# Feed-forward's second product in four chunks, by seven block products instead of eight, three of them kept in PSUM

## What is computed

```python
def rms_norm(x, g):
    xf = x.astype(jnp.float32)
    y = xf * lax.rsqrt(jnp.mean(xf * xf, axis=-1, keepdims=True) + EPS)
    return (y * g.astype(jnp.float32)).astype(x.dtype)
...
    x = x + rms_norm(merged @ w_o, norm_mix_post)
    hf = rms_norm(x, norm_ff_pre)
    ff = jnp.square(jax.nn.relu(hf @ w_ff_in)) @ w_ff_out
    return x + rms_norm(ff, norm_ff_post)
```

## Time and profile before

| what | us |
|---|---|
| median of 3 runs | 802.95 |
| the three runs | 802.93, 804.87, 802.95 |
| the profiled execution, its own time | 805.02 |
| the span of the trace in it | 803.3 |
| PE busy in the span | 790.7 (98%) |
| DVE busy | 415.5 (52%) |
| ACT busy | 322.2 (40%) |

### The profile page before, as it was taken

The page is one execution under the profiler, slowest core; times in us unless marked ns, Lnnn a source line. Parts: engine busy times, 40 slices in busy tenths (PEclk is TensorE's granted clock), DMA queues, the critical chain, the costliest instruction groups (busy, mean ns, idle before and its releaser), DMA issues.

```text
span 803.3 us, 10375 instructions
## 1 busy us (share of the span) xinstructions
PE 790.7 (98%) x3736; PEld 660.4 (82%) x3736; DVE 415.5 (52%) x730; ACT 322.2 (40%) x561; POOL 60.4 (8%) x110
## 2 busy tenths in 40 slices
PE   7999999999999999999999999999999999999996
PEld 6888888888887888888888988888888888888885
DVE  5624667777777238866536654442323354432334
ACT  4522656656565742232344444322112344322211
POOL 2000000122232003000002300000000000000001
PEclk8999999999999999999999999999999999999999
DMA  8243222212222631345231343322323333322202
GB/s 288 87 124 104 77 82 78 80 53 85 74 79 59 204 99 59 105 149 184 87 104 47 87 134 126 104 100 84 105 82 103 94 89 104 104 82 103 78 1 104
DMA packets 96214, 80.22 MB, mean 100 GB/s; under 512 B 3120, under 2 KB 77872, under 8 KB 96176
## 3 DMA queue, kind: packets, MB, share of 16 engines
q1 hardware_dynamic: 95504, 79.70, 31.6%
q10 hardware_dynamic: 672, 0.01, 0.0%
HBM read 77.60 MB, written 2.10 MB: 99 GB/s over the span
## 4 chain that ended last, share of the span: by engine, by line
PE 96%; DVE 2%; DMA 1%; ACT 1%; issue 0%; SPq 0%; DVEq 0%; POOLq 0%; POOL 0%; ACTq 0%
PE acc L1126 30%; PE acc L1127 30%; PE acc L1128 30%; PE aux L1313 1%; DMA g_pre<-in_norm_mix_pre 1%; PE aux L1239 1%; PE aux L1238 1%; PE aux L1248 1%; PE acc L1267 1%; PE acc L1264 1%; PE aux L1221 1%; PE aux L1168 1%; DVE x L819 0%; DVE actB_lo L810 0%; ACT probs L673 0%; DVE scores_sb L939 0%
## 5 line engine op out<-in xcount | busy, mean ns | idle before, releaser
L800 DVE TENSOR_TENSOR w_lo<-w_raw,w_hi 128x1024 fp32r<-128x1024 f32 x132 | 161.4, 1224 | 199.9 <-ACT w_hi L564 199.3
L564 ACT ACTIVATE w_hi<-w_raw 128x1024 fp32r<-128x1024 f32 x132 | 138.9, 1054 | 192.4 <-PE acc L1128 190.2
L1126 PE MATMUL acc<-actB_hi,w_hi 128*128 128x512 f32 (+1 forms) x544 | 207.0, 381 | 0.0
L1128 PE MATMUL acc<-actB_hi,w_lo 128*128 128x512 f32 (+1 forms) x544 | 205.2, 377 | 0.0
L1127 PE MATMUL acc<-actB_lo,w_hi 128*128 128x512 f32 (+1 forms) x544 | 205.0, 377 | 0.0
L1128 PEld LDWEIGHTS acc<-actB_hi,w_lo 128*128 128x128 f32 x544 | 102.4, 188 | 19.1
L1127 PEld LDWEIGHTS acc<-actB_lo,w_hi 128*128 128x128 f32 x544 | 102.5, 188 | 18.2
L1126 PEld LDWEIGHTS acc<-actB_hi,w_hi 128*128 128x128 f32 x544 | 102.4, 188 | 18.1
L1126 PE MATMUL acc<-w_hi,ff_hi 128*128 128x512 f32 x256 | 101.0, 395 | 0.0
L1128 PE MATMUL acc<-w_hi,ff_lo 128*128 128x512 f32 x256 | 101.0, 395 | 0.0
L1127 PE MATMUL acc<-w_lo,ff_hi 128*128 128x512 f32 x256 | 101.0, 394 | 0.0
(11 more groups left out here) (163 smaller groups left out, 895.9 us busy)
## 6 DMA issues: line engine op xcount, KB each, us to landing
w_raw<-in_w_in SPq DMA_DIRECT2D x44, 512.0 KB, 3.8
w_raw<-in_w_ff_in SPq DMA_DIRECT2D x32, 512.0 KB, 4.0
w_raw<-in_w_ff_out SPq DMA_DIRECT2D x32, 512.0 KB, 3.7
w_raw<-in_w_b SPq DMA_DIRECT2D x8, 512.0 KB, 3.5
w_raw<-in_w_a SPq DMA_DIRECT2D x8, 512.0 KB, 3.5
w_raw<-in_w_o SPq DMA_DIRECT2D x8, 512.0 KB, 3.7
x<-in_x SPq DMA_DIRECT2D x4, 512.0 KB, 7.5
x<-in_x SPq DMA_DIRECT2D x1, 2048.0 KB, 8.3
```

The source lines that it names most:

```text
L564: nc.scalar.activation(w_hi[:, j], w_raw[:, j], ACT.Copy).then_inc(hi_made, 1)
L800: nc.vector.tensor_tensor(w_lo[:, j], w_raw[:, j], w_hi[:, j].bitcast(F32), ALU.subtract).then_inc(lo_made, 1)
L1126: nc.tensor.matmul(o, a_hi, b_hi, start=first, stop=False)
L1128: return nc.tensor.matmul(o, a_lo, b_hi, start=False, stop=last)
```

## The change

**The products.** The second product is cut into 2 x 2 blocks: the tokens in two halves (0 to 255, 256 to 511), the inner dimension into even and odd tiles of 128, the output columns in two halves. With A for the activations and B for `w_ff_out`, the seven products are

- P1 = A11 B11, P2 = A12 B21, P4 = A22 T4, P3 = S4 B22
- P5 = S1 T1, P6 = S2 T2, P7 = S3 T3
- S1 = A21 + A22, S2 = S1 - A11, S3 = A11 - A21, S4 = A12 - S2
- T1 = B12 - B11, T2 = B22 - T1, T3 = B22 - B12, T4 = T2 - B21

and every output block is a sum of some of them. The S and T are made by DVE. The sums S, 256 wide per pair of tiles, lie in `s_raw`; their rounded and rest parts go to `op_hi` (in the region where `actA` and then `ff_sum` lay) and `op_lo` (in the region of `ff_hi` and `ff_lo`). T1, T2 and T4 lie in `t_raw`, which is slots 2 and 3 of `w_raw`; T3 overwrites B12 in `down_raw`.

**The chunks.** The 32 tiles go in four chunks of eight. A chunk is eight units of `w_ff_in` as before, and then the seven products in the order of `PRODUCTS`, each as two items (h = 0, 1) of 12 matmuls. Units and items share the ring of four slots of `w_hi` and `w_lo`; the numbers n = 0 to 21 are the 22 entries of a chunk. `w_ff_in` is now loaded into slots 0 and 1 of `w_raw` alone, and `w_ff_out` for a chunk as four transfers of 1 MB into `down_raw`.

**PSUM.** P5, P7 and P3 keep their two banks each over all four chunks. P1, P6, P4 and P2 share banks 0 and 1 of `acc` with each other and, from the second chunk on, with the `w_ff_in` units. Each of the four is taken out once a chunk (semaphore `taken`): by ACT copies in the first, by DVE additions in the second and third, by the merges in the last.

The diff, cut to its core:

```diff
@@ -76,9 +76,33 @@
...
-HALF_K = FF // P // 2
-U_HALF = 2 * HALF_K
-UNITS = U_FF + 2 * U_HALF
...
+CHUNKS = 4
+FF_UNITS = FF // P // CHUNKS
+PAIRS = FF_UNITS // 2
+PRODUCTS = ["P1", "P5", "P6", "P7", "P4", "P3", "P2"]
+ITEMS = FF_UNITS + 2 * len(PRODUCTS)
+UNITS = U_FF + CHUNKS * ITEMS
+LEFT = {"P1": 0, "P2": 1, "P4": 2, "P5": 3, "P6": 4, "P7": 5, "P3": 6}
+ROTATING = ["P1", "P6", "P4", "P2"]
+SUMS = ["T1a", "T1b", "T3a", "T2a", "T2b", "T3b", "T4a", "T4b"]
...
-            for c in range(2):
-                first = U_FF + c * U_HALF
-                with sp.Fori(0, HALF_K // SLOTS) as i:
-                    for j in range(SLOTS):
-                        slot_free(i * SLOTS + (first + j))
-                        load_columns(j, w_ff_in_v, bass.ds(i * (SLOTS * P) + (c * HALF_K + j) * P, P))
...
-                    for n in range(HALF_K // 2):
-                        slot_free(h * (HALF_K // 2) + (first + HALF_K + n))
-                        load_rows(n % SLOTS, w_ff_out_v, c * HALF_K + 2 * n, bass.ds(h * COL, COL))
...
+            def load_up(m):
+                if m < SLOTS:
+                    slot_free(U_FF + m)
+                else:
+                    before = m - 4 if m < 6 else m - 2
+                    sp.wait_ge(lo_made, U_FF + ff_unit(before) + 1)
+                load_columns(m if m < SLOTS else m % 2, w_ff_in_v, slice(m * P, (m + 1) * P))
+
+            def load_down(c, j):
+
+                if c:
+                    sp.wait_ge(lo_made, U_FF + item(c, 0))
+                elif j >= 2:
+                    sp.wait_ge(turned, T_FF + TT)
+                k = c * FF_UNITS + 2 * j
+                sp.dma_start(down_raw[:, j], w_ff_out_v[:, k:k + 2, :]).then_inc(down_loaded[j], 16)
...
+            for c in range(1, CHUNKS):
+                for n in range(FF_UNITS):
+                    load_up(c * FF_UNITS + n)
+                    if 2 <= n < 2 + PAIRS:
+                        load_down(c, n - 2)
...
+            for c in range(CHUNKS):
+                for n in range(FF_UNITS):
+                    m, j = c * FF_UNITS + n, n // 2
+                    act.wait_ge(pe_done, UNIT_DONE[U_FF + item(c, n)])
+                    if m >= 4:
+                        act.wait_ge(op_lo_made, 3 * ((m - 4) // 2 + 1))
+                    bank = n % (4 if c == 0 else 2)
+                    nc.scalar.activation(ff_act[:, m % 4], acc[:, bank], ACT.Relu).then_inc(relu_made, 1)
+                    hi_ahead(item(c, n))
+                    act.wait_ge(sq_made, m + 1)
+                    if n % 2 == 0:
+                        nc.scalar.activation(op_hi[:, j, 0], ff_act[:, m % 4, 0:2 * P],
+                                             ACT.Copy).then_inc(op_hi_made, 1)
+                    else:
+                        nc.scalar.activation(op_hi[:, j, 1:3].rearrange("p a s -> p (a s)"), ff_act[:, m % 4],
+                                             ACT.Copy).then_inc(op_hi_made, 1)
+                        act.wait_ge(s_made, 4 * (c * PAIRS + j + 1))
+                        nc.scalar.activation(op_hi[:, j, 3:7].rearrange("p a s -> p (a s)"),
+                                             s_raw[:].rearrange("p a s -> p (a s)"),
...
-                                                 ).then_inc(ssq_act, 1)
-                        if h == 0:
-                            for j in range(SLOTS):
-                                hi_of(UNITS - SLOTS + j)
+                        hi_ahead(product_item(c, name, h))
...
+                o, x, y = {"T1": (t, b12, b11), "T3": (b12, b22, b12), "T2": (t, b22, t), "T4": (t, t, b21)}[name[:2]]
...
+                for n in range(FF_UNITS):
+                    m, j = c * FF_UNITS + n, n // 2
+                    f = ff_act[:, m % 4]
+                    dve.wait_ge(relu_made, m + 1)
+                    nc.vector.tensor_tensor(f, f, f, ALU.mult).then_inc(sq_made, 1)
+                    lo_ahead(item(c, n))
+                    dve.wait_ge(sq_made, m + 1)
+                    if n % 2 == 0:
+                        if m >= 2:
+                            dve.wait_ge(op_hi_made, 3 * (c * PAIRS + j))
+                        nc.vector.tensor_tensor(s_raw[:, 2], f[:, 0:2 * P], f[:, 2 * P:S],
+                                                ALU.subtract).then_inc(s_made, 1)
+                        if n == 2:
+                            weight_sum(c, "T1a")
+                        if n == 4:
+                            weight_sum(c, "T1b")
+                        if n == 6:
+                            weight_sum(c, "T3a")
+                        if n == 0 and last:
+                            dve.wait_ge(taken, 8 * c)
+                            merge(sum2[:], sum2[:], sum1[:])
+                            merge(sum6[:], sum6[:], sum1[:])
+                        dve.wait_ge(op_hi_made, 3 * (c * PAIRS + j) + 1)
+                        nc.vector.tensor_tensor(op_lo[:, j, 0], f[:, 0:2 * P], op_hi[:, j, 0].bitcast(F32),
+                                                ALU.subtract).then_inc(op_lo_made, 1)
+                        if n == 6:
...
+                        e = ff_act[:, (m - 1) % 4]
+                        count = 4 * (c * PAIRS + j)
+                        nc.vector.tensor_tensor(s_raw[:, 0], e[:, 2 * P:S], f[:, 2 * P:S],
+                                                ALU.add).then_inc(s_made, 1)
+                        dve.wait_ge(s_made, count + 2)
+                        nc.vector.tensor_tensor(s_raw[:, 1], s_raw[:, 0], e[:, 0:2 * P],
+                                                ALU.subtract).then_inc(s_made, 1)
+                        dve.wait_ge(s_made, count + 3)
+                        nc.vector.tensor_tensor(s_raw[:, 3], f[:, 0:2 * P], s_raw[:, 1],
+                                                ALU.subtract).then_inc(s_made, 1)
+                        dve.wait_ge(op_hi_made, 3 * (c * PAIRS + j) + 2)
+                        nc.vector.tensor_tensor(op_lo[:, j, 1:3].rearrange("p a s -> p (a s)"), f,
+                                                op_hi[:, j, 1:3].rearrange("p a s -> p (a s)").bitcast(F32),
+                                                ALU.subtract).then_inc(op_lo_made, 1)
+                        dve.wait_ge(op_hi_made, 3 * (c * PAIRS + j) + 3)
+                        dve.wait_ge(s_made, count + 4)
+                        nc.vector.tensor_tensor(op_lo[:, j, 3:7].rearrange("p a s -> p (a s)"),
+                                                s_raw[:].rearrange("p a s -> p (a s)"),
+                                                op_hi[:, j, 3:7].rearrange("p a s -> p (a s)").bitcast(F32),
+                                                ALU.subtract).then_inc(op_lo_made, 1)
...
+                for name in PRODUCTS:
+                    for h in range(2):
+                        at = FF_UNITS + 2 * PRODUCTS.index(name) + h
+                        for made in {8: ["T2b"], 9: ["T3b"], 10: ["T4a"], 11: ["T4b"]}.get(at, []):
+                            weight_sum(c, made)
+                        lo_ahead(item(c, at))
+                    if 0 < c and not last and name in ROTATING:
+                        dst = {"P1": sum1, "P6": sum6, "P4": sum4, "P2": sum2}[name]
+                        for p in range(2):
+                            bank_done(name, p)
+                            nc.vector.tensor_tensor(dst[:, p], acc[:, p], dst[:, p], ALU.add).then_inc(taken, 1)
...
+                    if name == "P1":
+                        merged_so_far()
+                        for p in range(2):
+                            bank_done(name, p)
+                            merge(sum2[:, p], acc[:, p], sum2[:, p])
+                            merge(sum6[:, p], acc[:, p], sum6[:, p], signal=taken)
...
+                    if name == "P3":
+                        for p in range(2):
+                            bank_done(name, p)
+                            merge(sum1[:, p], aux[:, 2 + p], sum1[:, p], signal=ff_ready)
+                        for p in range(2):
+                            gain(4 + p, sum1[:, p], 1, p)
+                        for t in (2, 3):
+                            dve.wait_ge(rstd_ff, t - 1)
+                            dve.wait_ge(gained, 4)
+                            nc.vector.scalar_tensor_tensor(x1[:, t], down_raw[:, t, 0], rstd[:, 4, t:t + 1], x1[:, t],
+                                                           ALU.mult, ALU.add).then_inc(y_made, 1)
...
+            for p in range(2):
+                dve.wait_ge(pe_done, BANK_DONE[UNITS - 1, p])
+                nc.vector.tensor_tensor(sum2[:, p], acc[:, p], sum2[:, p], ALU.add).then_inc(ff_ready, 1)
+                gain(6 + p, sum2[:, p], 0, p)
+                dve.wait_ge(rstd_ff, 3 + p)
...
+            BANKS = {"P1": acc[:, 0:2], "P6": acc[:, 0:2], "P4": acc[:, 0:2], "P2": acc[:, 0:2],
+                     "P5": acc[:, 2:4], "P7": aux[:, 0:2], "P3": aux[:, 2:4]}
+
+            def bank_free(c, name, p):
+
+                if name in ROTATING:
```

(33 more changed lines are left out.)

349 lines of the change are left out of this document (215 added, 134 removed).

## The result

The changed kernel takes 811.03 us (median of four runs, 810.79 to 811.57). The kernel before takes 802.98 us beside it: ratio 1.0095, 95% interval 1.0078 to 1.0113. The forecast was 806.4 us in a range of 796.0 to 813.0. So the time lies inside the range and on the side that had the larger chance, but the loss is 8.05 us where +3.4 was forecast.

A forecast was written before the change was run, and what follows sets the result against it. PE was taken to bound the kernel, so each matmul less saves its time and each wait costs its length: -24.8 + 3.6 + 14.8 + 5.5 + 4.3 = +3.4 us, 802.95 + 3.4 = 806.4 us, range 796.0 to 813.0.

The forecast's parts named there:

- The unit stage is covered: Unit stage: DVE's last op_lo is ready 6.7 us after the odd unit, its first user starts at 8.2; no wait.
- the saving: Second product: 96 fewer matmuls give 22.3 us, the stationary operand's place 2.5; 24.8 us in all (22.3 to 26.1).
- the queueing: Between chunks: the fourth unit's load lands behind a 1 MB transfer, making the waits 14.8 us instead of 11.05.
- landing at E + 2.3: Between chunks: the next chunk's fourth unit's load lands 2.3 us after E, the end of P2.
- the waits between chunks: After P2, PE waits for its bank, whose taking stands behind the fourth unit's load: 5.4 + 5.4 + 4.0 = 14.8 us.
- ahead of P6: PE waits for P1's banks, taken late by DVE: 1.0, 1.0 and 1.6 us in chunks two to four, 3.6 us.
- the clock: Behind the waits between chunks PE falls to 1.2 GHz: 2.2, 2.2 and 1.1 us lost, 5.5 us (0 to 9.6).
- the end: After PE's last matmul DVE still has a queue: 10.8 us to the end instead of 6.5, 4.3 us more.
- The first: Rival: between chunks the loads do not queue (11.05 us) and the clock holds; faster, 797.1 us; chance 0.24.
- the second: Rival: no change, since only the clock holds behind the waits; 800.9 us; chance 0.17.
- The third: Rival: clock falls after each wait, 9.6 us, no gain from operand place; decides past some 3.5 us; 813.0 us; chance 0.17.
- The fourth: Rival: DVE bounds the unit stage, each pair of units growing by 1.2 us; about 819.6 us; chance 0.07.

The follow-up runs named there:

- the repeat: The changed kernel run once more without an edit (also the undisturbed profile): 810.00 us.
- the kernel with all changes: Changed kernel with P2's and P1's banks taken first, 1 MB loads two units later, op_hi and op_lo side by side, tail reordered: 785.84 us.

## Why the prediction was right or wrong

**Right: what would bind.** The unit stage is covered, all waits lie where the prediction put them, and each is ended by the instruction that it named. It put the saving and the loss in the right order of size, each over 20 us. The taking behind a foreign load was the cause of 14.8 + 5.6 of the 30.4 us that were lost again, shown by moving it.

**Right: the queueing.** 2.75, 4.15 and 4.15 us without and 4.0, 5.4 and 5.4 with the 1 MB ahead; measured 2.71, 4.08, 3.99 and, in the undisturbed profile, 4.32, 5.47, 5.51. A price from one row of 10.2 us held within 0.35 us a place.

**Wrong: the landing, and that it is one number.** The mechanism was right and two terms were mis-sized; this is the larger in the profile of the changed kernel. The step is "landing at E + 2.3", in the term for the waits between chunks. Between chunks two and three it was E + 4.8, and the term became 17.9 instead of 14.8: 3.1 of the 3.8 us by which the sum was short. The other profiles show it as scatter to the late side, in half of the cases at two of three places, which a sum of single durations leaves out. Undisturbed the landing was late too, E + 2.6 to 2.8 (five places in two profiles): the prediction's own row has 1.1 us from the end of the data to the landing for a load alone, and its sum took 0.6.

The scatter does not carry the miss alone. The repeat, without a late landing, is 1.0 us faster in the median (810.0 against 811.0) and still 3.6 above the forecast. Its terms are 23.2 for the saving, 3.0 ahead of P6, 15.8 between chunks, 6.6 for the clock and 3.9 for the end, which is +6.1: 1.6 us above the forecast's terms by the saving, 1.1 by the clock, 1.0 by the waits between chunks.

**Wrong in size: the saving.** This is the other mis-sized term, and it is short by the same 1.6 us in both profiles. "Two of three matmuls use `op_hi`, so I take 2.5 us" shared out the 0.0057 us by number (the earlier trace rows give 0.0054). Two tiles of three in region_a give 672 x (0.2324 - 0.2311) = 0.9 us, so 23.2 instead of 24.8. The place matters, as supposed, but its price doesn't go by share: one tile from region_b lengthens two distances of three.

**The clock: right in sum, by luck in its parts.** 5.5 forecast, 5.6 measured (6.6 in the repeat). The parts were 2.2, 2.2 and 1.1 for full falls behind the long pauses and half a fall behind the short one. In fact it fell behind each: 3.1, 6.0 and 2.9 us of PE's work lay in the low stretches, 1.5, 2.8 and 1.4 us lost. Pauses of 2.7 to 7.7 us were followed by the low clock in each of the 12 cases looked at (four profiles of three); those of up to 1.6 us, in the kernels with the taking first, in none. At about 10 us, ahead of the transposes, one of 2.26 us was not followed by it (the kernel with all changes) and one of 2.36 was (the kernel before). The Trainium skill says in "TensorE: Matmul & The Clock Gate", section "Part 1: The HAM clock gate (the "warmup" mystery)", that the clock is set by how busy the array has been of late. By that rule such a pause costs PE more than its length, and the trace agrees: 5.6 us beside 17.4 us of pauses.

**The smaller terms** held: P6 3.0 for 3.6, the end 3.9 for 4.3. DVE reaches P1's bank 11.07 us after P1's start, as the 11.1 said, though by luck: 6.7 and four steps of 1.14 are 11.3. The wait is shorter because PE arrives at 11.09 and not at 10.9, with its matmuls 0.2311 us apart. For the end, the last matmul before began at 796.55; 796.72 is the start of a piece of the chain, which changes nothing in the sum.

**What stays open** are 0.6 us of the difference between the profiled executions, 0.8 between the medians, that no row shows.

**The rivals.** The first and the second needed the clock to hold, and the first short waits as well; neither came. The third took 9.6 us for the clock and no gain in cadence; measured are 5.6 (6.6 in the repeat) and 0.9. Its bound, a pause of some 3.5 us, was too high: 2.7 was enough. The fourth, DVE as the bound, is out: PE waits nowhere in a unit stage.

## What to carry to other kernels

Before a change that reuses a buffer sooner, ask what stands in the queue in front of the instruction that frees it: here a copy of some 1 us stood behind a transfer for a unit that PE needed only 16 us later, and the wait and the low clock behind it ate 20 of the 23 us that 96 matmuls fewer gave; moving it in front gave the 20 us back. If a step waits for a transfer that isn't its own, move the step before anything else; clearing the queue ahead of the transfer gave 8 us first, and 0.6 once the order was right. Give the sum an end on the late side for each landing that PE waits for.

## What the runs showed of the hardware

- The stationary tile's place in SBUF moves the distance between matmuls of 512 columns from 0.2269 to 0.2324 us, by 2.4%, whichever tile lies there; one tile in three from the slower place lengthens two distances of three. The Trainium skill says in "TensorE: Matmul & The Clock Gate", section "Step-by-step: what each phase is for", that PE reads the two operands through separate ports, so that loading a tile takes nothing from the running matmul. That rule alone gives the place of a tile no price. Here it has one, and what region_b's reads meet is open.
- The low clock behind a pause lasted 3.4, 6.8 or 10.2 us, and not in step with the pause: 3.4 behind one of 5.5 us in one profile, 6.8 behind one of 5.5 us in the next.
- The same load at the same place was rounded 5.5 us after issue in one execution and 7.8 in another, when 1 MB was queued ahead of it; without that it landed after 3.9 to 4.1 us in all nine cases.
